# Second block's mixers: the fill products in three rounded products over 16 pieces of 256 columns

## The chip, the cores and the metric

The kernel is one program on one NeuronCore of a Trainium2 chip; the other cores of the chip do nothing. The metric is the device time of one execution in microseconds (us), as the median of several runs. Engines are named as the profile names them: PE multiplies matrices (PEld is its loading of the stationary operand), DVE is the vector engine, ACT the activation engine, POOL the general one, and SP issues the transfers from HBM.

## The reference, cut to what matters

A first block of two layers (convolution or attention, each with experts) is followed by a second block, twice: a feed-forward layer, a mixer, and a feed-forward layer, on 256 tokens of width 1024. The change lies in the mixer. Its input projection has 6328 columns; of these the columns for `nsa_q`, for `sk, sv, wk, wv` and for `merge_gate` (512 + 512 + 3072 = 4096 columns) are what the kernel calls the fills.

```python
def second_block(x, ...):
    for l in range(DEPTH):                      # DEPTH = 2
        x = x + 0.5 * swiglu_ffn(x, ffn1_norm[l], ffn1_wi[l], ffn1_wo[l])
        h = rms_norm_2(x, mix_norm[l])          # 256 x 1024
        (sb_q, sb_k, sb_v, mla_cq, mla_ckv, mla_kr, nsa_q, ck, cv, sk, sv, wk, wv,
         nsa_gate, merge_gate) = jnp.split(h @ w_in[l], offsets, axis=-1)
        o_sb = stick_breaking_attention(sb_q, sb_k, sb_v)
        o_mla = mla_attention(mla_cq, mla_ckv, mla_kr, ...)
        o_nsa = nsa_attention(nsa_q, ck, cv, sk, sv, wk, wv, nsa_gate, ...)
        gates = jax.nn.sigmoid(merge_gate)      # 256 x 3 x 1024
        y = gates[0] * (o_sb @ proj_sb[l]) + gates[1] * (o_mla @ proj_mla[l]) + gates[2] * (o_nsa @ proj_nsa[l])
        x = x + y @ w_out[l]
        x = x + 0.5 * swiglu_ffn(x, ffn2_norm[l], ffn2_wi[l], ffn2_wo[l])
    return x
```

## The kernel before, in words

All data are float32. Most products of the second block are made in three "rounded" products (`mm3`): each operand is split into a high part, rounded to the format `F32R`, and a low part, which is the rest; PE adds high x high, high x low and low x high. ACT writes the high part of a weight piece with a copy (`cut` on ACT, L1699 in the profile) and DVE the low part with a subtraction (`cut` on DVE, L2232), each over 128 x 2048 elements; two pairs of buffers take turns. A few products, the fills among them, are plain float32 products (`mm`), which need no parts. All matmuls go through one helper and show as L870, all transposes as L874.

Weights come through a ring of slots of 1 MB (128 x 2048 float32) in SBUF. SP issues the loads in the order in which they are written down; a load waits until the last use of its slot is over. In the second block the ring has the seven slots 0 to 6; slot 7 (`nsa_slot`) holds queries and keys, slots 8 to 13 are lent to the layers as room.

A mixer (`mixer` in each engine's program) runs in this order. The normalised input is transposed into `hT` and multiplied in features (`mi`, 10 products of 24 matmuls) and tokens (4 products); DVE writes the parts `mx.hT_high`/`mx.hT_low` and also the whole, unsplit `hT` (`whole_hT`), which only the fills read. Then three streams of work with long chains of dependences are woven together on every engine by the generator `weave`: stick-breaking attention and the preparation of the MLA attention (here called stretch A, 1521 to 1602 us in layer 0), MLA attention and the compressed part of the NSA attention (stretch B, 1602 to 1683 us), and the NSA attention units (stretch C, 1683 to 1727 us). Then come the output products (`mo`).

The fills are the background of this weaving. They are 8 pieces of 512 columns for each of two token halves. PE does each product in four steps of two of its eight k-tiles, one step at each `next(fill)` or background turn, 64 steps in a mixer; each result is built in PSUM bank 7 alone, ACT copies it out (event `filled`), and PE waits for that copy before the next product begins. Each engine works in strict program order, so a fill step stands between the operations of the chains at places that the order of the generators fixes.

```python
def fillers():
    for n in range(8):
        for t in range(TT):
            if n + t: T.wait_ge(*(E.filled...))
            for s, (slot, *landed) in enumerate(slots):
                for k in range(4):
                    mm(psum[:, 7, :], hT[:, s * 4 + k, t * P:(t + 1) * P], slot[:, k * 512:(k + 1) * 512], ...)
                    if k % 2 and s + k < 4: yield
            yield
```

Of the kernel before, what the change touches and what calls it, by code (L numbers as in the profile page):

```python
# [15 lines left out]
P = 128  # L16
# [25 lines left out]
LENT = 6  # L42
LAST_SLOT = 13024
# [229 lines left out]
def build(nc, A, consts, n_col, n_row):  # L273
# [44 lines left out]

    busy_r = nc.alloc_sbuf_tensor_at("busy_r", [P, 512], F32R, offset=gates_at)
# [143 lines left out]
    mx.hT_high, mx.hT_low = a.take(KT, S, rounded=True), a.take(KT, S, rounded=True)  # L463
# [77 lines left out]
    E.hT_whole = Event(nc, "hT_whole", [(u, k) for u in (6, 9) for k in (0, 4, 5, 6, 1, 2, 3, 7)])  # L541
# [67 lines left out]
    E.fill = Event(nc, "fill", keys(2, 8, TT, 2))  # L609
    E.filled = Event(nc, "filled", keys(2, 8, TT))  # L610
# [32 lines left out]
    got = {}  # L643
# [14 lines left out]
    def parts(st, c, p):  # L658


        if st == "mi" and p == 0:
            return cut_bufs["ff", 0][0]
        return cut_bufs[st, c][(p + (st == "ff" and c % 2 == 0)) % 2]

# [31 lines left out]
    fill_cols = [C_NQ, C_SK] + [C_MERGE + br * D + n * 512 for br in range(3) for n in range(2)]  # L696
# [4 lines left out]
    def sync_program():  # L701
        own, lent = [*range(N_SLOT - LENT), N_SLOT], list(range(N_SLOT - LENT, N_SLOT))
        order, landed, owner = list(own), [0] * (N_SLOT + 1), [None] * (N_SLOT + 1)

# [85 lines left out]
        def mixer(layer):  # L790
            w = A["w_in_2"][layer]
            for i, c0 in enumerate(mi_features):
                piece("mi", layer, i, cols_chunk(w, c0, 2 * P))
# [63 lines left out]
        lend(own[:-2])  # L857
# [10 lines left out]
    def tensor_program():  # L868
# [77 lines left out]
        def to_hT(u, between=None, after=lambda k: None):  # L946
# [6 lines left out]
            if u >= 5:  # L953
# [8 lines left out]
                T.wait_ge(*(E.hT_whole if u in norm_of_mix else E.hT_dve).at(u, 0))  # L962
# [589 lines left out]
        def mixer(l):  # L1552
# [3 lines left out]
            for n in range(10):  # L1556
# [30 lines left out]
            T.wait_ge(*E.hT_whole.at(u, KT - 1))  # L1587
# [6 lines left out]
            def fillers():  # L1594
                for n in range(8):
                    slots = [got["fill", l, n, s] for s in range(2)]
                    for t in range(TT):
                        if n + t:
                            T.wait_ge(*(E.filled.at(l, n, 0) if t else E.filled.at(l, n - 1, 1)))
                        for s, (slot, *landed) in enumerate(slots):  # L1600
                            if t == 0:
                                T.wait_ge(*landed)
                            for k in range(4):
                                i = mm(psum[:, 7, :], hT[:, s * 4 + k, t * P:(t + 1) * P], slot[:, k * 512:(k + 1) * 512],
                                       s + k == 0, s * 4 + k == KT - 1)
                                if k == 3:
                                    i.then_inc(*E.fill.inc(l, n, t, s))
                                if k % 2 and s + k < 4:
                                    yield
                        filled[0] += 1  # L1610
                        yield
# [23 lines left out]
            for br in range(3):  # L1635
# [6 lines left out]
                if br == 1:  # L1642
                    T.wait_ge(*E.filled.at(l, 7, 1))
# [53 lines left out]
    def scalar_program():  # L1697
# [421 lines left out]

        def mixer(l):  # L2120
# [14 lines left out]
            for i2 in range(2):  # L2135
# [3 lines left out]
                if i2:  # L2139
                    C.preload_act_table(ACT.Sigmoid)  # L2140
# [8 lines left out]
            def fillers():  # L2149
                for n in range(8):  # L2150
                    for t in range(TT):
                        yield
                        yield
                        yield
                        C.wait_ge(*E.fill.at(l, n, t, 1))
                        dst = (mx.nq, mx.kv)[n][:, t, :] if n < 2 else mx.merge[:, (n - 2) // 2, t, n % 2 * 512:(n % 2 + 1) * 512]
                        af(dst, psum[:, 7, :], ACT.Copy).then_inc(*act.ev(E.filled, l, n, t))
                        filled[0] += 1
                        yield
# [9 lines left out]
            def nsa_squares():  # L2169
                while filled[0] < 2 * TT:  # L2170
                    next(fill)
                C.wait_ge(*E.filled.at(l, 1, 1))
# [57 lines left out]
    def vector_program():  # L2230
# [120 lines left out]
        def scaled_hT(u, high, low, scale):  # L2351
            for k in range(KT):
# [4 lines left out]
                if k == 0 and u in norm_of_mix:  # L2357
                    whole_hT(u, scale, (0,))

        def whole_hT(u, scale, ks):  # L2360
            for k in ks:
                ts(hT[:, k, :], psum[:, turned_in(u, k), 0:S], scale[:, k:k + 1]).then_inc(*dve.ev(E.hT_whole, u, k))
# [363 lines left out]
        def stick_breaking(l):  # L2726
            for n in range(4):
                yield
                V.wait_ge(*E.sb_z.at(l, n))
                tt(mx.sp, mx.sp, wide(K("strict"), 2), ALU.mult).then_inc(*dve.ev(E.sb_sp, l, n))  # L2730
                yield
# [6 lines left out]
                yield  # L2738
                if n == 2:
# [135 lines left out]
        def compressed(l):  # L2875
# [3 lines left out]
            for t in range(TT):  # L2879
# [7 lines left out]
                tt(mx.E, mx.E, deep(stat[:, 0:8], 32), ALU.subtract).then_inc(*dve.ev(E.cs_dve, l, t, "sub"))  # L2887
                yield
# [232 lines left out]
```

## Time and profile before

| what | value |
|---|---|
| time, median of 3 runs | 2705.61 us (2702.48 to 2707.21) |
| profiled execution: time, and span of its trace | 2703.13 us, 2701.8 us |
| PE busy, of the span | 2294.2 us (85%) |
| DVE busy, ACT busy | 1062.5 us (39%), 805.6 us (30%) |
| the two mixers' stretches A to C | 1521 to 1727 us, and 2234 to 2440 us |

The span is the time from the first to the last instruction in the trace; the 1.3 us between it and the execution's own time lie around it. All positions in the text are in us from the span's start. Layer 1 repeats layer 0 about 712 us later. Matmuls are pipelined, so the time for one is read from the starts of a run of them, not from the length of a single one.

### The profile page before, as it was taken

How to read it: one execution, taken by the hardware profiler on the slowest of the kernel's cores; microseconds unless marked ns; L12 is line 12 of the kernel's file. 1: busy time of each engine (PE TensorE's matmuls, PEld its weight loads, DVE VectorE, ACT ScalarE, POOL GpSimd, SP SyncE). 2: the span in 40 equal slices, each digit the busy share in tenths (PEclk: the TensorE clock that was granted, in tenths of full speed). 3: DMA queues.
4: the chain of work that ended last, by engine and by line, in shares of the span. 5: the costliest groups of instructions: out<-in, count | busy, mean ns of one | idle time of the engine just before them, and what ended most of it. 6: DMA issues, size and time to landing. Idle time of an engine off the chain costs nothing.

```text
span 2701.8 us, 28726 instructions
## 1 busy us (share of the span) xinstructions
PE 2294.2 (85%) x12062; PEld 1392.8 (52%) x12062; DVE 1062.5 (39%) x1662; ACT 805.6 (30%) x1178; POOL 49.8 (2%) x91
## 2 busy tenths in 40 slices
PE   7987666667877767666999999999999999998999
PEld 4632111113552111112888644678888885446887
DVE  2331000103651000103765523667567554246774
ACT  3321000002430000002444432544454344235543
POOL 0000000000000000000000030000000001200000
PEclk8999888888989888888999999999999999999999
DMA  9799999999649999999756432356566573225662
GB/s 381 300 370 421 421 421 421 421 421 373 249 156 410 421 421 421 421 421 362 200 191 169 163 109 94 125 145 189 192 176 187 187 198 115 94 78 153 171 191 78
DMA packets 329905, 705.23 MB, mean 261 GB/s; under 512 B 15889, under 2 KB 227089, under 8 KB 277552
## 3 DMA queue, kind: packets, MB, share of 16 engines
q1 hardware_dynamic: 329776, 703.40, 71.1%
q8 instruction: 95, 1.56, 0.2%
q14 instruction: 34, 0.28, 0.0%
HBM read 702.30 MB, written 1.05 MB: 260 GB/s over the span
## 4 chain that ended last, share of the span: by engine, by line
PE 63%; DMA 27%; DVE 5%; ACT 3%; issue 1%; SPq 1%; DVEq 0%; ACTq 0%
PE psum L870 60%; DMA ring<-in_moe_w_up 12%; DMA ring<-in_moe_w_down 6%; DMA ring<-in_moe_w_gate 6%; PE psum L874 3%; DVE arena L2232 1%; DMA arena<-in_moe_w_gate 1%; DMA arena<-in_moe_w_down 1%; DMA arena<-in_moe_w_up 1%; DVE lent_r L2232 1%; ACT ring L1699 1%; DMA ring<-in_ada_w 1%; ACT xn L1699 1%; SPq L712 1%; DVE arena L2243 0%
## 5 line engine op out<-in xcount | busy, mean ns | idle before, releaser
L870 PE MATMUL psum<-ring,arena 128*32 128x512 f32 (+2 forms) x3208 | 605.2, 667 | 240.7 <-DMA ring<-in_moe_w_up 88.0
L870 PE MATMUL psum<-lent_r 128*128 128x512 f32 (+1 forms) x3344 | 610.7, 345 | 3.0 <-DVE lent_r L2232 2.8
L870 PEld LDWEIGHTS psum<-lent_r 128*128 128x128 f32 x3344 | 524.4, 189 | 89.3 <-issue 6.8
L870 PEld LDWEIGHTS psum<-ring,arena 128*32 128x32 f32 (+2 forms) x3208 | 152.2, 127 | 667.9 <-issue 215.9
L2232 DVE TENSOR_TENSOR lent_r<-ring,lent_r 128x2048 fp32r<-128x2048 f32 (+1 forms) x158 | 347.0, 2197 | 206.2 <-ACT lent_r L1699 206.2
L1699 ACT ACTIVATE lent_r<-ring 128x2048 fp32r<-128x2048 f32 (+1 forms) x158 | 290.3, 1842 | 292.8 <-PE psum L870 216.3
L1699 ACT ACTIVATE arena<-psum 128x512 f32<-128x512 f32 (+2 forms) x103 | 55.5, 575 | 827.8 <-PE psum L870 782.7
L870 PE MATMUL psum<-ring,hT 128*128 128x512 f32 x512 | 243.1, 607 | 8.5 <-ACT ring L1699 5.5
L870 PE MATMUL psum<-lent_r,arena_r 128*128 128x512 f32 x1056 | 242.4, 391 | 0.0
L870 PE MATMUL psum<-arena 128*32 128x512 f32 (+6 forms) x648 | 195.3, 496 | 36.1 <-DMA arena<-in_moe_w_up 8.0
L870 PEld LDWEIGHTS psum<-lent_r,arena_r 128*128 128x128 f32 x1056 | 198.3, 188 | 43.2
L2232 DVE TENSOR_TENSOR arena<-psum,arena 128x512 f32<-128x512 f32 (+2 forms) x21 | 20.3, 978 | 506.5 <-PE psum L870 506.5
L870 PEld LDWEIGHTS psum<-ring,hT 128*128 128x128 f32 x512 | 90.6, 191 | 105.0 <-issue 84.7
L2246 DVE TENSOR_REDUCE arena<-psum 128x512 f32<-128x1024 f32 x88 | 107.8, 1225 | 82.7 <-PE psum L870 82.6
L870 PE MATMUL psum<-arena_r,lent_r 128*128 128x512 f32 (+1 forms) x576 | 126.6, 381 | 3.3 <-DVE lent_r L2232 1.9
L870 PEld LDWEIGHTS psum<-arena 128*32 128x32 f32 (+4 forms) x648 | 69.2, 166 | 107.5 <-issue 38.9
L2232 DVE TENSOR_TENSOR arena<-psum,gate_b 128x512 f32<-128x512 f32 x16 | 10.3, 686 | 280.6 <-PE psum L870 280.6
L870 PEld LDWEIGHTS psum<-arena_r,lent_r 128*128 128x128 f32 x576 | 102.7, 191 | 26.5 <-DVE lent_r L2232 3.3
L2243 DVE COPY arena<-psum 128x256 f32<-128x256 f32 (+5 forms) x96 | 49.9, 527 | 159.4 <-PE psum L874 106.3
L2232 DVE TENSOR_TENSOR arena_r<-ring,arena_r 128x2048 fp32r<-128x2048 f32 (+1 forms) x38 | 82.8, 2179 | 68.4 <-ACT arena_r L1699 68.3
L1699 ACT ACTIVATE arena_r<-arena 128x256 fp32r<-128x256 f32 x88 | 36.8, 418 | 210.5 <-DVE arena L2232 210.5
L1699 ACT ACTIVATE ring<-psum 128x512 f32<-128x512 f32 (+3 forms) x84 | 47.4, 578 | 166.1 <-PE psum L870 117.1
(185 smaller groups left out, 1650.9 us busy)
## 6 DMA issues: line engine op xcount, KB each, us to landing
ring<-in_moe_w_up SPq DMA_DIRECT2D x120, 1024.0 KB, 26.9
ring<-in_moe_w_gate SPq DMA_DIRECT2D x119, 1024.0 KB, 26.5
ring<-in_moe_w_down SPq DMA_DIRECT2D x112, 1024.0 KB, 26.9
ring<-in_ffn_wi SPq DMA_DIRECT2D x176, 512.0 KB, 5.1
ring<-in_w_in SPq DMA_DIRECT2D x46, 1024.0 KB, 5.1
ring<-in_ffn_wo SPq DMA_DIRECT2D x44, 1024.0 KB, 4.9
ring<-in_ada_w SPq DMA_DIRECT2D x43, 1024.0 KB, 10.3
arena<-in_moe_w_gate SPq DMA_DIRECT2D x9, 1024.0 KB, 26.2
```

What stands on the lines that cost most here:

```text
L712: Y.dma_start(view(slot_of[n]), src).then_inc(slot_sem[n], 16)
L870: return T.matmul(out, lhsT, rhs, start=start, stop=stop, **kw)
L874: return T.transpose(out, in_, ident[0:k, 0:k])
L1699: return C.activation(out, a, f, **kw)
L2232: return V.tensor_tensor(out, a, b, op)
L2243: return V.tensor_copy(out, a)
L2246: return V.tensor_reduce(out, a, AX.X, op)
```

## The change

- The fills become 16 pieces of 256 columns. Each piece is loaded whole (all eight k-tiles) into one slot, split into a high and a low part, and multiplied by `mm3` with the parts of `hT`, for both token halves into the two halves of bank 7. PE still has four steps for each piece, of four k-tiles (12 matmuls) each, 64 steps in all.
- ACT makes the high part (`fill_high`) one step into the piece before, into one of two buffers; DVE makes the low part in place in the slot (`fill_low`), at the same step number of a new background generator of its own; PE waits for it (`E.fill_low`). DVE's generator advances in the weaves' background turns, twice for each of the four rounds of `stick_breaking` and twice for each token half of `compressed`. The first pair stands before the weaving, the low part ahead of `mla_prepare` on DVE.
- ACT copies out both token halves of a piece at once, so the number of copies stays 16 in a mixer.
- `whole_hT` and the waits on it go away. `mx.hT_high` takes the place of `hT`, `mx.hT_low` lies in slot 4, the two buffers for high parts are slots 5 and 6.
- The ring of the second block is then slots 0 to 3. At the start of each mixer slots 5, 6 and 7 are added to it, and they leave it again after the last piece of `mi`; ACT and POOL wait for what was last in them (`given_back`).

The diff, cut to its core:

```diff
+SPLIT = 4
+FILLS, FILL_W = 16, 256
...
-    mx.hT_high, mx.hT_low = a.take(KT, S, rounded=True), a.take(KT, S, rounded=True)
+    split_at = N_SLOT - LENT - SPLIT
+    mx.hT_high, mx.hT_low = hT_r, own_r[:, split_at, :].rearrange("p (k s) -> p k s", k=KT)
+    mx.fill_high = [own_r[:, split_at + 1 + n, :] for n in range(2)]
...
         def fill_loads(layer, i):
-            for h in range(2):
-                load(("fill", layer, i, h), E.fill.at(layer, i, 1, h), half_chunk(A["w_in_2"][layer], h, fill_cols[i], 512))
+            for n in (2 * i, 2 * i + 1):
+                load(("fill", layer, n), E.fill.at(layer, n), cols_chunk(A["w_in_2"][layer], fill_cols[n], FILL_W))
...
@@ mixer, SP; extra holds slots 5, 6, 7 @@
+            order[:0] = extra
...
                 piece("mi", layer, 7 + h, *low_and_gates(w, h))
+            lend(own[:split_at])
+            given_back.append([owner[n] for n in extra])
...
-        lend(own[:-2])
+        lend(own[:split_at])
...
-                T.wait_ge(*(E.hT_whole if u in norm_of_mix else E.hT_dve).at(u, 0))
+                T.wait_ge(*E.hT_dve.at(u, 0))
...
-                elif n:
-
-                    T.wait_ge(*E.hT_whole.at(u, 3 + n))
...
@@ fillers, PE @@
-                for n in range(8):
...
+                for n in range(FILLS):
+                    w = (mx.fill_high[n % 2], rounded_slot(got["fill", l, n][0]))
+                    if n:
+                        T.wait_ge(*E.filled.at(l, n - 1))
+                    T.wait_ge(*E.fill_low.at(l, n))
                     for t in range(TT):
...
+                        tok = slice(t * P, (t + 1) * P)
+                        for k in range(KT):
+                            i = mm3(psum[:, 7, t * FILL_W:(t + 1) * FILL_W], (high[:, k, tok], low[:, k, tok]),
+                                    tuple(v[:, k * FILL_W:(k + 1) * FILL_W] for v in w), k == 0, k == KT - 1)
+                            if k == 3 or (k == 7 and t == 0):
+                                yield
+                    i.then_inc(*E.fill.inc(l, n))
+                    filled[0] += 1
+                    yield
...
@@ ACT @@
+        def fill_high(l, n):
+            slot, *landed = got["fill", l, n]
+            C.wait_ge(*landed)
+            C.wait_ge(*(E.fill.at(l, n - 2) if n >= 2 else given_back[l][n]))
+            af(mx.fill_high[n % 2], slot, ACT.Copy).then_inc(*act.ev(E.fill_high, l, n))
...
                 if i2:
+                    fill_high(l, 0)
                     C.preload_act_table(ACT.Sigmoid)
...
@@ fillers, ACT @@
+                for n in range(FILLS):
+                    yield
+                    if n + 1 < FILLS:
+                        fill_high(l, n + 1)
+                    yield
+                    yield
+                    C.wait_ge(*E.fill.at(l, n))
...
+                    af(out[:, :, c0:c0 + FILL_W], psum[:, 7, :].rearrange("p (t c) -> p t c", t=TT), ACT.Copy).then_inc(
+                        *act.ev(E.filled, l, n))
...
@@ DVE @@
-        def stick_breaking(l):
+        def fill_low(l, n):
+            slot = got["fill", l, n][0]
+            V.wait_ge(*E.fill_high.at(l, n))
+            tt(rounded_slot(slot), slot, mx.fill_high[n % 2].bitcast(F32), ALU.subtract).then_inc(*dve.ev(E.fill_low, l, n))
+
+        def stick_breaking(l, fill):
...
                 tt(mx.sp, mx.sp, wide(K("strict"), 2), ALU.mult).then_inc(*dve.ev(E.sb_sp, l, n))
+                next(fill, None)
                 yield
...
-            whole_hT(u, scale, (4, 5, 6))
...
-                        whole_hT(u, scale, (1, 2, 3, 7))
...
+            def fillers():
+                for n in range(1, FILLS):
+                    yield
+                    fill_low(l, n)
+                    yield
+                    yield
+                    yield
...
+            fill_low(l, 0)
+            fill = fillers()
             mla = mla_prepare(l)
             next(mla)
-            weave(iter(()), 0, (stick_breaking(l), STEPS_A[1]), (mla, STEPS_A[2]))
+            weave(fill, STEPS_A[0], (stick_breaking(l, fill), STEPS_A[1]), (mla, STEPS_A[2]))
...
-            weave(iter(()), 0, (attention(nsa_units, 12 + 12 * l, bufs=mx.bufs, after=after), 1))
+            weave(spaced(fill, SPACED), STEPS_C, (attention(nsa_units, 12 + 12 * l, bufs=mx.bufs, after=after), 1))
+            run(fill)
...
@@ nsa_prepare, POOL @@
             G.wait_ge(*E.ns_act.at(l, "squares"))
+            G.wait_ge(*given_back[l][2])
```

## Rows read from the trace of the kernel before

**Rows 1.** The page's busy times of the whole span, by engine.
```profile
PE 2294.2 (85%) x12062; PEld 1392.8 (52%) x12062; DVE 1062.5 (39%) x1662; ACT 805.6 (30%) x1178; POOL 49.8 (2%) x91
```

**Rows 2.** Busy times by stretch: A, B, C of layer 0 (last: clock, DMA).
```profile
core 0: us, PE busy (x) PEld busy (x) DVE busy (x) ACT busy (x) POOL busy (x), PEclk, DMA share, GB/s
1521.40:1602.00 80.60, 77.04 (x300) 39.82 (x298) 31.91 (x70) 34.42 (x53) 23.77 (x43) 1.00 0.30 100
1602.00:1683.30 81.30, 74.89 (x323) 38.38 (x321) 23.78 (x84) 18.61 (x51) 0.56 (x1) 1.00 0.26 84
1683.30:1727.40 44.10, 37.75 (x246) 22.50 (x245) 25.61 (x105) 27.93 (x84) 0.00 (x0) 0.96 0.33 118
```

**Rows 3.** Groups by form, PE, 1521 to 1720 us: the fills.
```profile
L870 PE MATMUL psum<-ring,hT 128*128 128x512 f32 x256 | 120.7, 604 | 4.3 <-ACT ring L1699 2.8 <-issue 0.7 <-ACT arena L1699 0.7
```

**Rows 4.** Timeline of PE: two fill steps, and the next start.
```profile
1536.32 3.60 PE L870 MATMUL psum<-ring,hT 128*128 128x512 f32 x8
1539.85 0.70 PE L870 MATMUL psum<-ring 64*128 64x256 f32 x4
```

**Rows 5.** Groups by form, PE, 1464 to 1521 us: rounded matmuls of 256 columns.
```profile
L870 PE MATMUL psum<-arena_r 128*128 128x256 f32 x192 | 23.2, 283 | 0.0
```

**Rows 6.** Groups by form, whole span: both parts of a piece, and weight loads.
```profile
L870 PEld LDWEIGHTS psum<-lent_r 128*128 128x128 f32 x3344 | 524.4, 189 | 89.3 <-issue 6.8 <-DVE lent_r L2232 1.9
L2232 DVE TENSOR_TENSOR lent_r<-ring,lent_r 128x2048 fp32r<-128x2048 f32 x144 | 330.0, 2292 | 204.4 <-ACT lent_r L1699 204.4
L1699 ACT ACTIVATE lent_r<-ring 128x2048 fp32r<-128x2048 f32 x144 | 276.2, 1918 | 205.6 <-PE psum L870 205.6
```

**Rows 7.** The instructions on hT: the whole copies, min/median/max ns.
```profile
L2236 DVE TENSOR_SCALAR hT<-psum,col_sb x16: 472/473/476, 1464.2 to 2184.4; 128x256 f32<-128x256 f32 x16
```

**Rows 8.** Timeline of DVE: where mla_prepare begins.
```profile
1520.39 0.69 DVE L2232 TENSOR_TENSOR xn<-ring 128x512 f32<-128x512 f32 x1
```

**Rows 9.** Timeline of PE: first fill step, and first MLA transposes.
```profile
1521.39 1.98 PE L870 MATMUL psum<-ring,hT 128*128 128x512 f32 x4
1525.10 0.88 PE L874 MATMUL psum<-const_sb,ring 128*128 128x128 f32 x6 [1.72 <-DVE ring L2232]
```

**Rows 10.** Timeline of ACT: stick-breaking's first exponential, and MLA's second exponentials' end.
```profile
1548.05 0.84 ACT L1699 ACTIVATE ring<-ring 128x768 f32<-128x768 f32 x1
...
1614.23 0.19 ACT L1699 ACTIVATION_READ_ACCUMULATOR ring<-ring,arena 128x1 f32 x1
```

**Rows 11.** Timeline of DVE: a mask product, and two products of probabilities.
```profile
1559.48 0.95 DVE L2232 TENSOR_TENSOR ring<-ring,const_sb 128x768 f32<-128x768 f32 x1
...
1611.57 0.69 DVE L2232 TENSOR_TENSOR ring<-ring 128x512 f32<-128x512 f32 x1
...
1668.97 1.23 DVE L2232 TENSOR_TENSOR ring<-ring 128x1024 f32<-128x1024 f32 x1
```

**Rows 12.** Timeline of PE: what reads those results, in the same order.
```profile
1549.91 0.87 PE L870 MATMUL psum<-ring 128*64 128x256 f32 x8
...
1562.69 0.70 PE L870 MATMUL psum<-ring 64*128 64x256 f32 x4
...
1618.30 0.60 PE L874 MATMUL psum<-const_sb,ring 128*128 128x128 f32 x4
...
1670.25 0.66 PE L874 MATMUL psum<-const_sb,ring 128*128 128x128 f32 x4 [0.93 <-DVE ring L2232]
```

**Rows 13.** Timeline of PE in the first block: attention units without fills.
```profile
743.86 1.14 PE L870 MATMUL psum<-arena 128*64 128x128 f32 x16 [1.35 <-ACT arena L1699]
...
748.84 2.03 PE L870 MATMUL psum<-arena 128*64 128x128 f32 x16 [0.69 <-ACT arena L1699]
```

**Rows 14.** The page's DMA issues: line, count, KB each, us to landing.
```profile
ring<-in_ffn_wi SPq DMA_DIRECT2D x176, 512.0 KB, 5.1
ring<-in_w_in SPq DMA_DIRECT2D x46, 1024.0 KB, 5.1
```

**Rows 15.** Timeline of ACT: high parts of two neighbouring feed-forward pieces.
```profile
1281.95 1.92 ACT L1699 ACTIVATE lent_r<-ring 128x2048 fp32r<-128x2048 f32 x1 [1.62 <-PE psum L870]
1287.54 1.92 ACT L1699 ACTIVATE lent_r<-ring 128x2048 fp32r<-128x2048 f32 x1 [0.56 <-PE psum L870]
```

More of the change, by code:

```diff
@@ L608, in build @@
     E.mi_dve = Event(nc, "mi_dve", keys(2, [("f", n) for n in range(0, 10, 2)] + [("t", n) for n in range(2)]))
-    E.fill = Event(nc, "fill", keys(2, 8, TT, 2))
-    E.filled = Event(nc, "filled", keys(2, 8, TT))
+    E.fill_high, E.fill_low = Event(nc, "fill_high", keys(2, FILLS)), Event(nc, "fill_low", keys(2, FILLS))
+    E.fill = Event(nc, "fill", keys(2, FILLS))
+    E.filled = Event(nc, "filled", keys(2, FILLS))
     E.busy = Event(nc, "busy_rows", keys(1))
@@ L642, in build @@
     act, dve, pool = Line(nc, "act"), Line(nc, "dve"), Line(nc, "pool")
-    got = {}
+    got, given_back = {}, []
     E.stored = nc.alloc_semaphore("s_stored")
@@ L663, in parts, with rounded_slot @@
         return cut_bufs[st, c][(p + (st == "ff" and c % 2 == 0)) % 2]
+    def rounded_slot(slot):
+        return own_r[:, next(n for n in range(split_at) if slot_of[n] is slot), :]
     def turned_in(u, k):
@@ L695, in build @@
     at_turns = [8, 9, 10, 11, 0, 1, 2, 3, 4, 5, 6, 7]
-    fill_cols = [C_NQ, C_SK] + [C_MERGE + br * D + n * 512 for br in range(3) for n in range(2)]
+    fill_cols = [c0 + n * FILL_W for c0, width in ((C_NQ, 512), (C_SK, 512), (C_MERGE, 3 * D)) for n in range(width // FILL_W)]
     mi_features = [C_SBQ, C_SBQ + 256, C_SBK, C_SBK + 256, C_CK]
@@ L791, in mixer @@
             w = A["w_in_2"][layer]
+            order[:0] = extra
+            if layer:
+                owner[extra[0]], owner[extra[1]], owner[extra[2]] = E.fill.at(0, FILLS - 2), E.fill.at(0, FILLS - 1), E.ns_pe.at(0, KT - 1)
             for i, c0 in enumerate(mi_features):
@@ L1642, in mixer @@
                 if br == 1:
-                    T.wait_ge(*E.filled.at(l, 7, 1))
+                    T.wait_ge(*E.filled.at(l, FILLS - 1))
                 for h in range(2):
@@ L2149, in fillers @@
             def fillers():
[L2150 to L2159, printed above, removed]
+                for n in range(FILLS):
[5 more added lines that the diff above has]
+                    C.wait_ge(*E.fill.at(l, n))
+                    out, c0 = ((mx.nq, 0), (mx.kv, 0), (mx.merge[:, 0], 0), (mx.merge[:, 0], 512), (mx.merge[:, 1], 0),
+                               (mx.merge[:, 1], 512), (mx.merge[:, 2], 0), (mx.merge[:, 2], 512))[n // 2]
+                    c0 += n % 2 * FILL_W
+                    af(out[:, :, c0:c0 + FILL_W], psum[:, 7, :].rearrange("p (t c) -> p t c", t=TT), ACT.Copy).then_inc(
+                        *act.ev(E.filled, l, n))
+                    filled[0] += 1
+                    yield
             def nsa_all():
@@ L2356, in scaled_hT @@
                     *dve.ev(E.hT_dve, u, k))
[L2357 to L2362, printed above, removed]
         def add_gated(st, which, u, banks=(0, 1, 2, 3)):
@@ L2738, in stick_breaking @@
                 yield
+                next(fill, None)
                 if n == 2:
@@ L2873, in nsa_prepare, with compressed @@
             yield
-        def compressed(l):
+        def compressed(l, fill):
             E4 = mx.E.rearrange("p (b a) n -> p b a n", b=2)
@@ L2887, in compressed @@
                 tt(mx.E, mx.E, deep(stat[:, 0:8], 32), ALU.subtract).then_inc(*dve.ev(E.cs_dve, l, t, "sub"))
+                next(fill, None)
                 yield
@@ L2900, in compressed @@
                 cp(mx.pT[0:32, :, :], psum[0:32, 4:6, :].rearrange("p b (h c) -> p (b h) c", h=4)).then_inc(*dve.ev(E.cs_dve, l, t, "pT"))
+                next(fill, None)
                 yield
```

28 lines of the change are left out of this document (7 added, 21 removed).

## The prediction

> **What bounds the kernel now.** The page's busy times come first: PE works 85% of the span, DVE 39%, ACT 30% [rows 1], so a product that PE does faster can shorten the kernel where PE is what the others wait for. Whether it is so in the mixers is read from the busy times by stretch [rows 2]. In A PE is busy 77.0 of 80.6 us, in B 74.9 of 81.3, in C 37.8 of 44.1; the clock granted is 1.00 in A and B and 0.96 in C, the higher of its two levels nearly throughout. DVE (31.9, 23.8, 25.6) and ACT (34.4, 18.6, 27.9) have time left in sum. In these stretches the fills are the largest piece of PE's work: 256 matmuls, 120.7 us with the ends of each run counted [rows 3]. So before, PE sets the pace in A and B, and the chains between PE, DVE and ACT lie hidden behind the fill steps, with 3.6 and 6.4 us of PE's time left idle. In C 6.35 of 44.1 us are idle, and the chain is near to the pace.
>
> **The products.** Eight fill matmuls take from 1536.32 to 1539.85 us: 3.53 / 8 = 0.441 us each [rows 4]; 256 of them make 113.0 us in a mixer. After the change there are 16 pieces x 2 token halves x 8 k-tiles x 3 = 768 rounded matmuls of 256 columns with a 128 x 128 stationary operand. The trace has that shape in `mi`: 192 in 23.2 us, 0.121 us each [rows 5], so 92.8 us. That saves 20.2 us in a mixer, 0.32 us in each of the 64 steps. It is the best that the change can give there; the least is nothing, where the chains set the pace.
>
> The Trainium skill (FP8 and Floating Point Precision, section TensorE Precision Notes) counts a true float32 product as four passes through the array. Three passes in place of four would leave 84.8 of the 113.0 us, an estimate from that page, and save 28.2 us in a mixer in place of 20.2. The rows disagree with it by 8 us, and the sum goes by the rows.
>
> **The copies that go.** `whole_hT` is 16 instructions of 0.473 us [rows 7], eight in a mixer. One stands ahead of the last transposes of `to_hT`; the other seven lie on DVE while PE multiplies features without a pause (the 192 matmuls of [rows 5] have no idle time before them). I take 0.4 us for the one; the bounds are nothing and 8 x 0.473 = 3.8 us.
>
> **What is added.** Each piece needs a high part on ACT, 1.92 us, and a low part on DVE, 2.29 us [rows 6]: 16 x 1.92 = 30.7 and 16 x 2.29 = 36.7 us in a mixer. In sum there is room: ACT would be busy 112 and DVE 118 of 206 us [rows 2]. What they cost is a matter of order, because both engines work in program order: `fill_low(n)` waits for `fill_high(n)` at the same step number on ACT, and all that stands behind it on DVE waits with it, the mask products of stick-breaking, the maxima and the probabilities of the attention, for which PE waits in turn. I go through the places, pricing each by what is late for PE.
>
> Opening: `fill_low(l, 0)` stands directly ahead of `mla_prepare` on DVE. That begins at 1520.39 us [rows 8] and leads to the transposes at 1525.10, before which PE is already idle 1.72 us [rows 9] with one fill step to do [rows 9]. The whole 2.29 us go to the path. The high part of piece 0 is not late: it is on ACT ahead of the last token product, and the slot's transfer takes 5.1 us [rows 14].
>
> Stretch A, pairs 1 to 5. `fill_high(2)` stands ahead of the first exponential, which ends at 1548.89 [rows 10]; PE uses it at 1549.91 [rows 12]. Spare 1.02 us; PE comes two steps, 0.64, earlier; 1.92 - 1.02 + 0.64 = 1.5 us. `fill_low(3)` stands ahead of the mask product that ends at 1560.43 [rows 11]; PE uses it at 1562.69 [rows 12]. Spare 2.26, three steps earlier: 2.29 - 2.26 + 0.96 = 1.0 us. I take their mean, 1.25, for each of the five: 6.3 us. The bounds are nothing and 5 x 2.29.
>
> Stretch B, pairs 6 to 13. For pair 8 the high part can begin after ACT's exponentials at 1614.42 [rows 10]; then 1.92 + 2.29 and the 0.69 of the probabilities give 1619.3 at the least, with 0.2 for the reciprocal 1619.5. PE used them at 1618.30 [rows 12] and comes four steps earlier: 1.2 + 1.28 = 2.5 us. Pair 13 stands ahead of the product that ends at 1670.20 [rows 11], for which PE waits 0.93 us already [rows 12]: 2.3 us. For the other six DVE stands waiting for PE, busy 23.8 of 81.3 us [rows 2]; I take nothing for them, and 2.29 each as the upper bound. Together 4.8 us.
>
> Stretch C, pairs 14 and 15. An attention unit without fills takes 4.98 us in the first block [rows 13], the eight units of C now 44.1 / 8 = 5.5 each [rows 2]. Of the nine steps' 2.9 us I take 1.2 to be kept and 1.7 lost; the bounds are 0 and 2 x 2.29 lost.
>
> Edits at nothing. ACT's copies of bank 7 are 16 in a mixer and of 512 elements before and after, and PE waits for them as often. The fills move the same 16 MB in 16 loads of 1 MB. The ring of four slots: a feed-forward piece takes 1287.54 - 1281.95 = 5.59 us [rows 15], a slot comes round after four, 22.4 us, less 4.2 for the two parts [rows 6] and 5.1 for the transfer [rows 14]: 13 us to spare on SP's queue. With that cover gone each of 33 pieces could cost up to 5 us. The first pieces of `mi` find slots 5 to 7 free in addition, as many as before. POOL's and ACT's waits on `given_back` are on products that end before the weaving begins.
>
> **The sum.** Per mixer: -20.2 - 0.4 + 2.3 + 6.3 + 4.8 + 1.7 = -5.5 us, twice -11.0. The profiled execution (2703.13) would come to 2692.1; it lies 2.5 us under the median, from which I count: 2705.6 - 11.0 = 2694.6 us. 0.2%, or 5.4 us, is about what a measurement of this kernel can tell from no change.
>
> **The rivals.**
> *The pairs hide.* DVE and ACT are idle half of A and B [rows 2], so all but the opening may disappear: 2 x (20.2 + 0.4 - 2.3) = 36.6 us faster, 2669 us. Against it: pairs 2, 3, 8 and 13 have less spare than they take.
> *Back to where it was.* Pairs 6 to 15 cost as much as the rest leaves, 20.6 - 2.3 - 6.3 = 12.0 us a mixer, 1.2 each: 2700 to 2711 us. Four of the places above are at or over that price.
> *The pairs set the pace.* The mechanism is the wait of `fill_low` for `fill_high` in DVE's order, in the attention of B and C. If each of the ten pairs there costs its whole 2.29 us, 22.9 + 2.3 + 6.3 - 20.6 = 10.9 us a mixer are lost: 2727 us. It decides the sign from 1.2 us a pair.
> *Weight loads.* Three loads now stand for each one. If in the fills they did not overlap the matmuls, each would take the 0.189 us of a load [rows 6]: 145.2 us against 113.0, and with the opening 34 us more a mixer, 2774 us. Against it, the 192 matmuls of [rows 5] have a load each and run at 0.121 us. The Trainium skill (TensorE: Matmul & The Clock Gate, section Back-to-back issue gap) has the spacing of a stream set by loads and matmuls together; the trace agrees as far as that the loads of that run are hidden.
> *The ring is too short.* Some first piece comes late: 2710 us or more.
>
> **How the numbers follow.** Forecast 0.46 (its own range 2684 to 2700), pairs hide 0.14, no change 0.22, pairs set the pace 0.12, weight loads 0.04, ring 0.02. Faster by over 0.2%: 0.46 + 0.14 = 0.60; within: 0.22; slower: 0.12 + 0.04 + 0.02 = 0.18. The range, 2672 to 2716, holds the forecast, no change, and some two thirds of the two cases beside them: 0.46 + 0.22 + 0.09 + 0.08 = 0.85.
>
> **What would show it.** Right: fill matmuls at 0.121 us in runs of 12; PE's first wait in A, for DVE, over 3 us in place of 1.72; the mixers' stretches A to C each about 5 us shorter than 206; PE's busy time there 20 us less, and its idle time, put down to DVE subtractions and ACT exponentials, up from 16 to about 31 us. Wrong: if that idle time stays under 20 us, the pairs hide; if it grows to over 37, they set the pace; if a run of 12 takes more than 1.6 us, the price of the products is off; if the feed-forward layers change their length, it is the ring.

## The result, and the profile after

The changed kernel takes 2717.2 us (median of 4 runs, 2714.2 to 2718.2) against 2704.7 us (4 runs): 1.0044 times the time before, 95% interval 1.0027 to 1.0061. It is slower by 12.5 us. The profiled execution took 2718.04 us with a span of 2716.7.

First the busy times of the whole span, to be held against [rows 1]. PE is busy 11.7 us less; DVE gained 65.8 and ACT 58.1 us.

```profile
PE 2282.5 (84%) x13086; PEld 1504.3 (55%) x13086; DVE 1128.3 (42%) x1678; ACT 863.7 (32%) x1210; POOL 59.7 (2%) x91
```

Then the stretches of the mixer in layer 0 and layer 1: the opening (up to the first MLA transposes), the rest of A, B and C, cut at the same instructions as in [rows 2] (the opening and the rest together are A).

```profile
core 0: us, PE busy (x) PEld busy (x) DVE busy (x) ACT busy (x) POOL busy (x), PEclk, DMA share, GB/s
1525.18:1531.24 6.06, 1.75 (x14) 1.48 (x13) 5.50 (x15) 2.48 (x5) 0.92 (x2) 1.00 0.00 0
1531.24:1610.75 79.51, 71.71 (x486) 59.69 (x486) 42.47 (x64) 44.67 (x56) 22.71 (x37) 0.96 0.33 100
1610.75:1697.46 86.71, 73.27 (x563) 66.93 (x561) 41.79 (x92) 31.41 (x59) 5.57 (x6) 0.90 0.29 92
1697.46:1739.59 42.13, 34.17 (x318) 28.47 (x317) 27.55 (x106) 29.41 (x85) 0.00 (x0) 1.00 0.29 101
...
2245.03:2251.10 6.07, 1.77 (x14) 1.49 (x13) 5.51 (x15) 2.49 (x5) 0.93 (x2) 1.00 0.00 0
2251.10:2327.98 76.88, 68.87 (x487) 57.16 (x487) 41.98 (x64) 44.67 (x56) 21.37 (x35) 1.00 0.34 104
2327.98:2413.66 85.68, 72.24 (x563) 66.14 (x561) 42.27 (x92) 31.42 (x59) 7.00 (x8) 0.92 0.30 92
2413.66:2455.79 42.13, 34.17 (x318) 28.47 (x317) 27.46 (x106) 29.41 (x85) 0.00 (x0) 1.00 0.30 101
```

A to C is 214.4 and 210.8 us long in place of 206.0 and 207.2 before: 6.0 longer in the mean, where 5 shorter was forecast. Two columns explain it. PE's idle time (length less busy) is 33.6 us where it was 16.7, which is close to the 31 of the forecast. But PE is busy 179.0 us, only 10.9 less than the 189.9 of before, and the granted clock, 0.98 to 1.00 in A and B before, is 0.90 to 0.96 in three of the four stretches. Layer 0 and layer 1 execute the same instructions in A with nearly the same idle time (7.80 and 8.01 us), and layer 0 is busy 2.84 us longer, at a clock of 0.96.

The rest is as before: the second block's other stages take 898.05 us against 898.20 between the same instructions. The first block, which the diff does not touch, ended 4.9 us later in this execution than in that of before. Among all the profiles used here the mixer of layer 0 begins between 1461.7 and 1466.8 us, whatever the kernel changes behind it, so lengths of stretches are the finer measure.

The timeline shows the waits. DVE, ACT and PE around the low part of piece 8 and around that of piece 13 (columns: start, us, engine, line, operation, tiles; in brackets the idle time before and what ended it):

```profile
1622.21 1.90 ACT L1710 ACTIVATE own_r<-ring 128x2048 fp32r<-128x2048 f32 x1
1624.14 2.29 DVE L2254 TENSOR_TENSOR own_r<-ring,own_r 128x2048 fp32r<-128x2048 f32 x1 [4.52 <-ACT own_r L1710]
1626.56 0.69 DVE L2254 TENSOR_TENSOR ring<-ring 128x512 f32<-128x512 f32 x1
1627.30 0.66 PE L891 MATMUL psum<-const_sb,ring 128*128 128x128 f32 x4 [1.82 <-DVE ring L2254]
...
1679.80 2.27 DVE L2254 TENSOR_TENSOR own_r<-ring,own_r 128x2048 fp32r<-128x2048 f32 x1
1681.99 0.16 DVE L2591 RECIPROCAL ring<-ring 128x4 f32<-128x4 f32 x1
1682.19 1.23 DVE L2254 TENSOR_TENSOR ring<-ring 128x1024 f32<-128x1024 f32 x1
1683.47 1.11 PE L891 MATMUL psum<-const_sb,ring 128*128 128x128 f32 x4 [3.43 <-DVE ring L2254]
```

For pair 8 the high part, the low part, the probabilities and the transposes stand in one line behind each other; for pair 13 it is the low part, the probabilities and the transposes. Both are as the prediction had them. What follows each wait it did not have. The same view of PE's fills at 1611 us and behind the wait of 3.43 us:

```profile
1611.21 0.40 PE L887 MATMUL psum<-own_r,hT_r 128*128 128x256 f32 x2
1611.45 0.28 PE L887 MATMUL psum<-own_r 128*128 128x256 f32 x1
1611.57 0.40 PE L887 MATMUL psum<-own_r,hT_r 128*128 128x256 f32 x2
...
1686.89 0.63 PE L887 MATMUL psum<-own_r,hT_r 128*128 128x256 f32 x2
1687.32 0.41 PE L887 MATMUL psum<-own_r 128*128 128x256 f32 x1
1687.53 0.63 PE L887 MATMUL psum<-own_r,hT_r 128*128 128x256 f32 x2
```

Three matmuls start within 0.36 us at 1611 and within 0.64 us at 1687. The busy times by 5 us around the two waits give the clock:

```profile
1620.00:1625.00 5.00, 4.97 (x42) 4.97 (x43) 0.86 (x1) 4.11 (x9) 0.00 (x0) 1.00 0.68 210
1625.00:1630.00 5.00, 3.18 (x21) 2.95 (x19) 2.21 (x3) 0.60 (x1) 0.00 (x0) 0.81 0.01 3
1630.00:1635.00 5.00, 4.31 (x23) 3.49 (x21) 2.26 (x2) 2.40 (x2) 0.00 (x0) 0.50 0.68 210
...
1680.00:1685.00 5.00, 1.16 (x5) 0.71 (x4) 3.71 (x4) 0.32 (x1) 0.00 (x0) 0.78 0.00 0
1685.00:1690.00 5.00, 4.67 (x24) 4.67 (x25) 0.00 (x0) 0.88 (x2) 0.00 (x0) 0.54 0.02 3
```

Behind each of these two waits PE works for some microseconds at the lower of its two levels, 1.2 GHz (0.50), and the fills there cost nearly twice their price.

### The profile page after: what moved, and what is told of

Read it like the earlier page. It is cut to its first block, busy times and chain, and to the rows that moved or that the text cites. A ratio compares the mean times of both kernels' runs of the same rounds, so it can differ in the third digit from the quotient of the medians.

```text
span 2716.7 us, 30866 instructions
## 1 busy us (share of the span) xinstructions
PE 2282.5 (84%) x13086; PEld 1504.3 (55%) x13086; DVE 1128.3 (42%) x1678; ACT 863.7 (32%) x1210; POOL 59.7 (2%) x91
## 4 chain that ended last, share of the span: by engine, by line
PE 59%; DMA 27%; DVE 7%; ACT 5%; issue 1%; SPq 1%; ACTq 0%; DVEq 0%
PE psum L887 57%; DMA ring<-in_moe_w_up 12%; DMA ring<-in_moe_w_down 7%; DMA ring<-in_moe_w_gate 5%; PE psum L891 2%; ACT ring L1710 2%; DVE own_r L2254 1%; DVE arena L2254 1%; DMA arena<-in_moe_w_gate 1%; DMA arena<-in_moe_w_down 1%; ACT own_r L1710 1%; DMA ring<-in_ada_w 1%; DVE lent_r L2254 1%; SPq L724 1%; ACT xn L1710 1%
## 5 line engine op out<-in xcount | busy, mean ns | idle before, releaser
L887 PE MATMUL psum<-own_r,hT_r 128*128 128x256 f32 x1024 | 208.3, 303 | 21.4 <-ACT ring L1710 17.5
L887 PEld LDWEIGHTS psum<-own_r,hT_r 128*128 128x128 f32 x1024 | 167.3, 201 | 33.4 <-ACT ring L1710 18.8
L887 PE MATMUL psum<-own_r 128*128 128x256 f32 x512 | 149.5, 292 | 0.0
L887 PEld LDWEIGHTS psum<-arena 128*32 128x32 f32 (+4 forms) x648 | 69.4, 167 | 96.7 <-issue 29.6
L887 PE MATMUL psum<-arena_r,lent_r 128*128 128x512 f32 x480 | 114.4, 399 | 3.3 <-DVE lent_r L2254 1.9
L887 PEld LDWEIGHTS psum<-arena_r,lent_r 128*128 128x128 f32 x480 | 90.8, 190 | 26.4 <-DVE lent_r L2254 3.3
L1710 ACT ACTIVATE arena_r<-arena 128x256 fp32r<-128x256 f32 x88 | 36.8, 418 | 210.4 <-DVE arena L2254 210.4
L887 PEld LDWEIGHTS psum<-own_r 128*128 128x128 f32 x512 | 102.8, 201 | 0.0
## 6 DMA issues: line engine op xcount, KB each, us to landing
ring<-in_moe_w_up SPq DMA_DIRECT2D x120, 1024.0 KB, 26.7
ring<-in_moe_w_down SPq DMA_DIRECT2D x112, 1024.0 KB, 26.7
```

Source lines behind the costliest of these rows:

```text
L887: return T.matmul(out, lhsT, rhs, start=start, stop=stop, **kw)
L1710: return C.activation(out, a, f, **kw)
```

## The experiments

In the texts below TensorE, VectorE, ScalarE and GpSimd are PE, DVE, ACT and POOL of the profile. Each run was timed in 3 or 5 rounds beside the kernel before, whose median was 2704.8 to 2706.9 us in the four groups of runs. "Length" and "idle" are those of A to C, mean of both mixers, from the windows of each run's one profile; busy is the difference. A single profile can lie some way off the median of its run: that of `halves_early` is of the slowest of five executions, 2698.5 us.

| run | us | ratio to before, 95% | length | PE idle | PE busy |
|---|---|---|---|---|---|
| before | 2704.7 | 1 | 206.6 | 16.7 | 189.9 |
| changed | 2717.2 | 1.0027 to 1.0061 | 212.6 | 33.6 | 179.0 |
| products_only | 2678.6 | 0.9882 to 0.9909 | 192.2 | 18.7 | 173.5 |
| high_only | 2684.3 | 0.9911 to 0.9937 | 196.2 | 22.2 | 174.0 |
| low_only | 2697.4 | 0.9964 to 0.9985 | 204.1 | 25.7 | 178.4 |
| plain_products | 2734.5 | 1.0092 to 1.0120 | 222.2 | 25.5 | 196.7 |
| ring_of_four | 2706.5 | 0.9988 to 1.0006 | 206.6 | 16.7 | 189.9 |
| kept_busy | 2711.7 | 1.0003 to 1.0027 | 209.8 | 24.9 | 184.8 |
| low0_early | 2712.2 | 1.0013 to 1.0032 | 210.4 | 31.5 | 178.9 |
| high_early | 2706.1 | 0.9993 to 1.0011 | 207.0 | 28.8 | 178.3 |
| low_on_pool | 2714.9 | 1.0023 to 1.0048 | 211.5 | 32.1 | 179.4 |
| pool_and_low0 | 2709.3 | 1.0008 to 1.0026 | 209.1 | 29.6 | 179.5 |
| halves | 2706.0 | 0.9990 to 1.0008 | 207.7 | 27.5 | 180.2 |
| early_and_low0 | 2703.0 | 0.9982 to 1.0000 | 207.7 | 26.7 | 181.0 |
| halves_early | 2692.0 | 0.9943 to 0.9973 | 204.2 | 24.6 | 179.7 |
| halves_late | 2694.9 | 0.9951 to 0.9978 | 204.1 | 25.7 | 178.4 |
| halves_mixed | 2689.1 | 0.9931 to 0.9955 | 198.8 | 23.7 | 175.1 |
| mixed_busy | 2690.3 | 0.9918 to 0.9957 | 200.9 | 19.0 | 182.0 |

**Products alone.**

```
- w = (mx.fill_high[n % 2], rounded_slot(got["fill", l, n][0]))
+ w = (mx.fill_high[0], mx.fill_high[0])   # fill_high(l, 0) only, no fill_low
```

> Leaves out the parts: only piece 0's high part is made, and all sixteen pieces are multiplied with it (as both operands), so the fills hold other numbers; loads, order, products and copies out of bank 7 stay. Theory A (the parts' waits, and the lower clock that follows them): without parts the waits go, the granted clock stays at 1.00 in the mixers' stretches A and B, a step of 12 matmuls takes 1.45 us, and the kernel takes 2704.7 - 2 x (16 to 20) = 2665 to 2673 us. Theory B (three rounded products in the woven order are not cheaper than the true float32 one): a step takes over 1.6 us and the kernel 2695 us or more.

Measured 28 us faster than before (2706.9 us in its group): the products do gain, so theory B falls, but less than theory A's 32 to 40. The time lies in neither range. The stretches of layer 0:

```profile
1525.27:1529.13 3.86, 1.69 (x14) 1.49 (x13) 3.44 (x13) 2.48 (x5) 0.92 (x2) 1.00 0.00 0
1529.13:1601.15 72.02, 69.61 (x487) 58.66 (x487) 28.63 (x58) 32.14 (x49) 20.87 (x38) 0.98 0.36 110
1601.15:1674.91 73.76, 66.54 (x564) 60.90 (x562) 23.78 (x84) 18.62 (x51) 2.77 (x5) 1.00 0.34 108
1674.91:1717.00 42.09, 35.02 (x318) 29.21 (x317) 25.17 (x105) 27.72 (x84) 0.00 (x0) 0.96 0.30 101
```

Busy time falls by 16.4 us a mixer and idle time grows by 2.0. Against this run the changed kernel has the same number of matmuls, 14.9 us more idle time, and 5.5 us more busy time. More busy time for the same matmuls points to the clock, and the granted clock gives about the same sum: 1 less the clock, times the length, is 9.4 us a mixer over the stretches of the changed kernel and about 4 over those of this run. That is an estimate, as if PE worked all the while.

**Parts with the old price of products.**

```
- i = mm3(psum[...], (high, low), w, k == 0, k == KT - 1)
+ i = mm(psum[...], high.bitcast(F32), w[0].bitcast(F32), k == 0, k == KT - 1)
```

> Makes both parts of every piece at the same places, but multiplies high part by high part in one true float32 product, 256 columns wide (the low parts are waited for and not used). Theory A (waits grow because PE reaches its operands earlier): PE spends its old 113 us a mixer on the fills, the parts are mostly hidden behind them, and what is left is the opening's 2.3 us and some 2 to 5 us more a mixer: 2704.7 + 2 x (4 to 7) = 2713 to 2719 us, with a granted clock of 1.00 in A and B. Theory C (the parts delay the chains by the same whatever the products take, 17 us of idle time a mixer as in the changed kernel): 2704.7 + 2 x 17 = 2739 us.

Measured between the two, nearer to theory C. Idle time grew by 8.8 us, not 17: with slower steps about half of what the parts bring does not show. That speaks for theory A's mechanism, but its 4 to 7 us were too few, and neither theory had the 6.8 us more of busy time. It goes with the float32 product in twice as many matmuls and a clock of 0.96 and 0.94 in B; how it divides between them is not shown.

**The ring.**

```
- lend(own[:-2])
+ lend(own[:4])        # and slots 5, 6, 4 first in order for the mixer's first pieces
```

> The kernel before with nothing but the ring of four slots (from the feed-forward layer on, with three slots lent to the first pieces of the mixer). All theories but one: no change, 2702 to 2707 us. If the short ring is what costs the 12 us: 2710 us or more, in the feed-forward layers or in the first pieces of the mixer.

Measured no change. The rival of the short ring is out.

**High part and low part one at a time.** `high_only` is the changed kernel without `fill_low`, multiplying `(high, high)`. `low_only` makes one high part a mixer and subtracts that from every piece, so VectorE never waits for ScalarE.

> Leaves out the low parts: every high part is made on ScalarE at its place, and the three products use it as both operands (the fills hold other numbers); VectorE does nothing for the fills. Against the run with products alone (2679 us): if ScalarE's high parts in its order cost little, 2679 to 2687 us; if they are half of the parts' price, 2690 to 2698; if they are most of it, above 2700.

> Leaves out the high parts but that of piece 0, which all pieces use: VectorE subtracts it from each piece at the places of the changed kernel, without a wait for ScalarE (the fills hold other numbers). If VectorE's subtractions in its order are the price, with no help from their wait for ScalarE: 2700 to 2710 us; if that wait is a third or more of it (moving the high parts forward brought 11 us): 2690 to 2700; if VectorE's part is small: under 2690.

Above products alone, the high parts cost 5.7 us and the low parts 18.8 us; both together, in the changed kernel, 38.5. So 14.0 us are in neither and come only with both. By the lengths of the mixers it is 2 x 4.0, 2 x 11.9 and 2 x 20.4, which leaves 9.0; in idle time a mixer 3.5, 7.0 and 14.9, which leaves 4.4. What the two runs lack and the changed kernel has is the wait of `fill_low` for `fill_high`; the next runs test it. `high_only` is in the first of its three cases, `low_only` in the middle one.

**High parts a step earlier, and piece 0's low part earlier.**

```
  for n in range(FILLS):
-     yield
      if n + 1 < FILLS:
          fill_high(l, n + 1)
      yield
+     yield
...
- fill_low(l, 0)                     # ahead of mla_prepare
...
+     else:                          # ahead of the wait for the last token product
+         fill_low(l, 0)
```

> The changed kernel with each high part one step earlier on ScalarE (first step of a piece in place of its second), so that VectorE's subtraction finds it done; in the changed kernel VectorE stood 16.9 us in layer 0 waiting for high parts, in 7 places. If that wait is what makes the chains late (the mechanism of the rival that was called the pairs set the pace): 4 to 8 us less idle time a mixer, 2700 to 2710 us. If the length of the two operations in their engines' order is what costs: no more than 1 us a mixer either way, 2713 to 2720.

> The changed kernel with the low part of piece 0 moved on VectorE from ahead of the MLA preparation to ahead of the last copy of the token products, where VectorE waits for TensorE anyway. If the price of the opening (2.3 us a mixer) was put right: PE's idle time there falls from 4.31 to about 2.1 us and the kernel takes 2717 - 2 x 2.2 = 2712 to 2713 us, some 1 to 2 us less if the clock then stays up at the start of stretch A. If the opening was not on the path: no change, 2715 to 2719.

> High parts one step earlier and the low part of piece 0 early. If the two gains (11 us and 5 us against the changed kernel) are of different places and add up: 2700 to 2703 us. If they overlap: 2704 to 2707.

The step forward alone gains 11.1 us: the wait of 1.82 us behind piece 8's low part is gone, that of 3.43 behind piece 13's stays, because VectorE did not wait for its high part in the changed kernel either. The early low part gains 5.0 us; the opening's idle time goes from 4.31 to 2.17 us. Together they gain 14.2, nearly the sum (16).

**Low parts on GpSimd.**

```
+ for n in range(1, 6):              # GpSimd, ahead of nsa_prepare; 8 to 15 behind it
+     fill_low(layer, n)
```

> The changed kernel with 13 of the 16 low parts of a mixer on GpSimd in place of VectorE (pieces 0, 6 and 7 stay on VectorE, since GpSimd prepares NSA's queries and keys meanwhile). If the subtractions in VectorE's order are what delays the chains: the waits for VectorE in B and C and the late maxima go, 6 to 9 us of idle time a mixer, and part of the lower clock with them, 2690 to 2704 us. If ScalarE's high parts delay them as much, or GpSimd is too slow (its product of 128 x 512 takes 1.14 us here, so an estimated 4.6 us for a low part) and PE waits for the low parts themselves: 2712 us or more.

> The two edits together: low part of piece 0 early on VectorE, 13 low parts on GpSimd. If their gains add up: that of the run with GpSimd less another 4 to 6 us, 2686 to 2700 us, below the kernel before (2705 to 2707). If the second mechanism (high parts in ScalarE's order) then shows: 2700 to 2712.

The gains of the first cases did not come: 2.3 us, and 7.9 with the early low part. Both times lie in the second ranges, but not for the reasons given there alone. GpSimd needs 4.6 us for a low part, as estimated, and PE waits for one only twice (3.1 us in layer 0). Part of what undid the gain stands in the timeline at the compressed attention and at the same probabilities as above:

```profile
1665.52 4.58 POOL L3048 TENSOR_TENSOR own_r<-ring,own_r 128x2048 fp32r<-128x2048 f32 x1 [8.87 <-ACT own_r L1713]
1666.97 3.43 DVE L2257 TENSOR_TENSOR arena<-arena,stat 128x256 f32<-128x256 f32 x1
...
1672.50 0.42 DVE L2257 TENSOR_TENSOR arena<-arena,stat 128x256 f32<-128x256 f32 x1
1673.21 4.55 POOL L3048 TENSOR_TENSOR own_r<-ring,own_r 128x2048 fp32r<-128x2048 f32 x1 [3.10 <-ACT own_r L1713]
1674.07 1.21 DVE L2268 COPY arena<-psum 32x1024 f32<-32x1024 f32 x1 [1.14 <-PE psum L894]
...
1675.40 3.43 DVE L2257 TENSOR_TENSOR ring<-ring 128x1024 f32<-128x1024 f32 x1
1678.89 1.12 PE L894 MATMUL psum<-const_sb,ring 128*128 128x128 f32 x4 [3.42 <-DVE ring L2257]
```

A VectorE product that takes 0.42 us alone takes 3.43 us and ends just behind GpSimd's subtraction. The probabilities, 1.23 us before, take 3.43 too. PE's wait of 3.42 us is as long as with the low part on VectorE.

**The clock.**

```
  yield
+ stay_busy(8, 4)                    # eight rounded matmuls on constants
  T.wait_ge(*E.ml_dve.at(l, "low"))
```

and three like it, behind stick-breaking's third product and behind the two parts of the compressed attention.

> The changed kernel with four groups of eight rounded matmuls of 512 columns on constants in each mixer, ahead of four of PE's long waits: the MLA transposes (3.07 us in the changed kernel), the fill piece behind stick-breaking's third product (2.57), the fill piece behind the first part of the compressed attention (2.71), and the probabilities of the MLA unit behind its second part (3.43). They write banks that nobody reads then; the waits themselves stay. If the lower clock behind those waits is a cost of its own (PE busy 3 us longer in A of layer 0 and 4 to 5 us in B than at 1.00): granted clock 1.00 behind them and 2717 - (6 to 13) = 2704 to 2711 us. If the clock goes down whatever PE does there, or the low clock is only where PE waits anyway: 2715 to 2722.

Measured 5.5 us faster than the changed kernel, just above the first case and well under the second, with 64 matmuls more. A and B of both layers:

```profile
1530.60:1607.48 76.88, 70.89 (x494) 58.57 (x495) 42.01 (x64) 44.66 (x56) 21.37 (x35) 1.00 0.34 104
1607.48:1690.65 83.17, 73.61 (x580) 66.74 (x578) 42.20 (x92) 31.41 (x59) 6.98 (x8) 0.96 0.30 95
...
2246.70:2323.44 76.74, 70.83 (x496) 58.51 (x494) 41.83 (x64) 44.51 (x56) 21.26 (x34) 1.00 0.34 104
2323.44:2407.56 84.12, 74.57 (x580) 67.43 (x578) 42.21 (x92) 31.41 (x59) 6.98 (x8) 0.94 0.30 94
```

A of layer 0 runs at 1.00 and is 2.6 us shorter than in the changed kernel; A of layer 1, which was at 1.00 already, keeps its length within 0.2 us. B is 3.5 and 1.6 us shorter, at 0.96 and 0.94 in place of 0.90 and 0.92. All that although PE does more. So the lower clock is a cost of its own, and it is smaller where PE is kept at work; it does not vanish in B. The run's eleven executions lie in two groups, four at 2700 to 2705 us and seven at 2710 to 2714, and the profile is of one of the seven; what sets the four apart stays open.

**Halves.** Each part in two instructions of 1024 columns, PE waiting for the first half at its first step and for the second at its second.

```
- tt(rounded_slot(slot), slot, ...).then_inc(*dve.ev(E.fill_low, l, n))
+ half = slice(h * 1024, (h + 1) * 1024)
+ tt(rounded_slot(slot)[:, half], slot[:, half], ...).then_inc(*dve.ev(E.fill_low, l, n, h))
```

`halves_early` adds both high halves at the first step and piece 0's low part early; `halves_late` moves the low halves one step back; `halves_mixed` does so from piece 7 on only; `mixed_busy` adds the constants' matmuls.

> The changed kernel with each part made in two halves of 1024 columns at two neighbouring steps (high halves at the first and second step of a piece, low halves at the second and third), and PE waiting for the first half at its first step and for the second at its second. Theory A (length of one insertion sets the wait, and a long wait lowers the clock): an insertion is some 1.0 to 1.2 us in place of 1.9 to 2.3, waits of over 2 us become rare, the clock stays near 1.00, 2685 to 2700 us. Theory D (what counts is the work put in DVE's and ACT's order in sum, however it is cut): 2712 to 2720 us.

> Both parts in halves of 1024 columns, both high halves at the first step of a piece, low halves at its second and third, the low part of piece 0 early. If the length of an insertion and the wait of VectorE for ScalarE's high parts are separate costs: 2690 to 2699 us. If both cure the same waits: 2699 to 2705.

> As the run before, with the low halves one step later (third and fourth step of a piece). If VectorE gains room when the low part stands behind the attention's maxima and probabilities: 2685 to 2697 us. If PE then waits for the low parts themselves: 2700 us or more.

> Halves with both high halves at the first step and piece 0 early, as in the best run so far (2692 us), but the low halves of pieces 7 to 15 one step later than those of pieces 1 to 6. By the lengths of the stretches in the two runs (A 77.6 against 81.4 to 81.8 us, B 80.1 against 77.1, C 42.6 against 41.2 to 41.7): 3.9 to 4.4 us a mixer better, 2683 to 2686 us. If a late piece in B only passes its wait on: 2689 to 2695.

> The run before with the four groups of matmuls on constants, six each. If the lower clock still costs something with short waits (clock 0.94 to 0.96 in A and B of the best run so far): 2 to 8 us below the run before. If the waits are too short for that work: the same or up to 6 us above it.

Halving alone gains 11.1 us and takes 6.1 us of idle time a mixer away. The 2706.0 us lie in neither range. Theory D falls, since cutting the same work does gain. Theory A is not borne out either: the clock in A and B is 0.94 to 0.95, and layer 0 still has four waits of over 2 us (4.20 in the opening, 2.28, 2.25 and 2.36), as many as the changed kernel (3.07, 2.57, 2.71 and 3.43). `halves_early` and `halves_late` are in their first cases. Late low halves lose 4 us in A and gain 3 in B. `halves_mixed` takes the better place in each and has the lowest median, 0.57% under before, though its interval overlaps that of `halves_early`. By its time it is at the edge of the second case, though its stretches came out as the first had them (A 77.6 and 76.1, B 77.2 and 75.7, C 41.7 us). The profile of `halves_early`, from which those were forecast, lies 6.5 us over its run's median, that of `halves_mixed` 1.1. With the matmuls on constants no gain shows: idle time falls by 4.7 us a mixer, busy time grows by 6.9, and the six executions spread from 2677.5 to 2695.2 us.

## Why the prediction was wrong

**What failed** is the step called the products, with its premise from the first part that the clock of 1.00 in A and B would stay. The sum has no term for a clock that the new waits lower, which measured 5.5 us a mixer, and the products themselves gave 16.4 us in place of 20.2. Per mixer, mean of both, against the sum:

| term | predicted | measured | from |
|---|---|---|---|
| products, as PE's busy time | -20.2 | -16.4 | products_only against before |
| idle time that comes back without any part | in the next terms | +2.0 | same |
| parts: opening 2.3, A 6.3, B 4.8, C 1.7 | +15.1 | +14.9 | idle, changed against products_only |
| lower clock | 0 | +5.5 | busy, same two runs |
| `mi` and `whole_hT` | -0.4 | -0.9 | 58.6 and 58.7 us against 59.7 and 59.4 |
| sum | -5.5 | +5.1 | |

Twice 5.1 is 10.2 us. The other 2.3 us of the 12.5 lie within what the first block's end moves from run to run.

- *The products.* Mis-sized. Eight float32 matmuls took 3.53 us [rows 4]; 24 rounded ones, from 1610.75 to 1613.72 us, take 2.97: 0.124 us each, and 0.28 in place of 0.32 us saved a step, 17.9 us. The other 1.5 us go with the clock of 0.93 to 0.98 that some stretches have even without the parts.
- *The lower clock.* Missing, and it decides the sign: without its 5.5 us the sum is -0.4 us a mixer, about no change, while with the products at their forecast size and this clock it is still +1.3. The prediction counted each wait once. In the changed kernel PE pays again behind some of them. The Trainium skill (TensorE: Matmul & The Clock Gate, section HAM oscillation) describes a kernel whose waits between groups of matmuls throttle PE again, so that the next group starts at the lower clock. That speaks against this change, and the prediction did not weigh it. The trace agrees: 0.50 to 0.54 behind the waits of 1.82 and 3.43 us, and a higher clock where PE was kept at work (0.96 to 1.00 in A of layer 0, 0.90 and 0.92 to 0.96 and 0.94 in B). The waits in that section are on transfers; here one of 1.82 us on VectorE was followed by the same.
- *The parts.* Right in sum, and that in part by luck: B was put 1.4 us too low, the other places together 1.6 too high. By place: the opening 2.1 of 2.3; A 5.4 of 6.3 (pair 2 made PE wait 1.34 us, 1.5 predicted; pair 3 0.49 at the place that was priced, 1.0 predicted); B 6.2 of 4.8; C 1.2 of 1.7. Behind the opening the longest wait in A is at pair 5, 2.57 us, which the mean of pairs 2 and 3 put at 1.25: it is 0.66 in products_only and in low_only and 2.13 in high_only, so most of it is the high part's place on ACT. Pair 8 was put at 2.5 and waits 1.82; pair 13 at 2.3 and its wait grew from 0.93 to 3.43 (1.23 in products_only). The miss in B is one of the six pairs taken at nothing: piece 11's low part stands ahead of an attention unit's maxima. The exponentials come late, ACT's copy of bank 7 stands behind them, and PE waits 2.71 us for the copy (0.51 in products_only). The lines show pair 5 (high part, the mask product that comes late, PE's wait) and then pair 11:

```profile
1585.06 1.91 ACT L1710 ACTIVATE own_r<-ring 128x2048 fp32r<-128x2048 f32 x1
...
1591.63 0.95 DVE L2254 TENSOR_TENSOR ring<-psum,const_sb 128x768 f32<-128x768 f32 x1
...
1596.95 0.50 PE L887 MATMUL psum<-own_r,hT_r 128*128 128x256 f32 x2 [2.57 <-ACT ring L1710]
...
1658.55 2.27 DVE L2254 TENSOR_TENSOR own_r<-ring,own_r 128x2048 fp32r<-128x2048 f32 x1
1660.75 0.41 DVE L2565 CUSTOM_DVE_ANT_0 ring<-psum,const_sb 128x256 f32<-128x256 f32 x1
...
1664.78 0.57 ACT L1710 ACTIVATE ring<-psum 128x512 f32<-128x512 f32 x1
1665.40 0.58 PE L887 MATMUL psum<-own_r,hT_r 128*128 128x256 f32 x2 [2.71 <-ACT ring L1710]
```

- *The rivals.* The wait of `fill_low` for `fill_high`, the mechanism of "the pairs set the pace", is real: moving the high parts a step gains 11.1 us, though their new place on ACT is in that gain too. But it is not the whole price of ten pairs, and the idle time stayed under the 37 us set for that case. *The pairs hide* is out, since the idle time rose to 33.6 us and did not stay under 20. Weight loads and ring are out (products_only, ring_of_four). A run of 12 is under the 1.6 us of the test at full clock (half of 2.97 us) and over it behind the waits, where three matmuls take 0.64 us: that test did point at the products, by way of the clock.

How far the clock loss follows from each single wait stays open: layer 1 of the changed kernel kept 1.00 through A with the same waits with which layer 0 fell to 0.96.

## What to carry to other kernels

When work moves off the bounding engine onto engines that were "half idle", price it by place: what stands behind each inserted instruction in program order, and who waits for that. Then ask what the new waits do to TensorE's clock, since here waits of 1.8 to 3.4 us were in part paid again in slower matmuls behind them. The same work can be made to pay: cut into halves, with the high part a step ahead and the first piece where VectorE waited anyway, it went from 0.44% slower to 0.57% faster.

## What the runs showed of the hardware that was not expected

The granted clock fell to 0.50 behind waits of 1.82 and 3.43 us in an otherwise busy stretch, for an estimated 7 us each by the rows of 5 us above (0.81 and 0.50; 0.78 and 0.54), and one and the same program kept it in one layer and lost it in the other (A: 1.00 and 0.96).

While GpSimd subtracted two SBUF tiles (4.58 us), VectorE's products of two SBUF operands took 3.43 us in place of 0.42 (256 columns) and 1.23 (1024 columns); VectorE's copy out of PSUM shortly before the second of them kept its usual 1.21 us while GpSimd worked. The Trainium skill (SBUF — State Buffer, section SBUF: two separate sides) states that the two engines share a port pair, which one instruction holds to its end, and that VectorE needs it for two SBUF inputs. The trace agrees. The changed kernel has the other order too: in layer 1 GpSimd's product of 128 x 512, begun at 2328.89 us while VectorE subtracted a low part (2328.44 to 2330.96), took 2.97 us in place of 1.04.
